# The softmax reciprocal is multiplied in on GpSimd instead of VectorE, in the attention of layer 0

## The reference

```python
s = where(valid, q @ k.T * dh ** -0.5 - slope * distance, NEG_INF)
p = exp(s - max(s));  den = sum(p);  o = (p @ v) / den     # per dilation group
out = sum over groups of softmax(m + log(den)) * o         # merged per head
```

## Time and profile before

| | |
|---|---|
| median of 3 runs | 1867.74 us |
| the profiled execution | 1868.67 us, span 1867.0 us |
| PE, PEld | 1716.0 us (92%), 1388.2 us (74%) |
| DVE, ACT, POOL | 1372.9 us (74%), 1087.9 us (58%), 51.4 us (3%) |
| mean granted TensorE clock | 0.973 |
| the units of the first half, of the second | from 173 to 215 us, from 325 to 370 us of the span |

### The profile page before, as it was taken

The page is one execution under the profiler, slowest core; times in us unless marked ns, Lnnn a source line. Parts: engine busy times, 40 slices in busy tenths (PEclk is TensorE's granted clock), DMA queues, the critical chain, the costliest instruction groups (busy, mean ns, idle before and its releaser), DMA issues. The chain is left out here.

```text
span 1867.0 us, 25871 instructions
## 1 busy us (share of the span) xinstructions
PE 1716.0 (92%) x9941; PEld 1388.2 (74%) x9941; DVE 1372.9 (74%) x1236; ACT 1087.9 (58%) x1074; POOL 51.4 (3%) x100
## 2 busy tenths in 40 slices
PE   0998998899999998989898999999999999999996
PEld 0997898679999875656676776767677766788784
DVE  4557556667776668559678887987988688898885
ACT  2344443553333345457766677777767678767773
POOL 2000000001111000000000000000000000000000
PEclk9998999899999999988899999999999999999998
DMA  9866177038887622249878998988999899999992
GB/s 298 300 236 227 58 259 261 11 123 284 311 293 260 226 83 88 84 156 360 314 288 312 336 357 296 394 317 319 364 342 365 293 351 359 385 346 340 364 346 90
DMA packets 244300, 503.84 MB, mean 270 GB/s; under 512 B 10296, under 2 KB 82144, under 8 KB 244192
## 3 DMA queue, kind: packets, MB, share of 16 engines
q1 hardware_dynamic: 228688, 451.44, 67.8%
q0 software_dynamic: 13824, 50.34, 7.3%
q10 hardware_dynamic: 1680, 0.60, 0.2%
HBM read 501.29 MB, written 1.05 MB: 269 GB/s over the span
## 5 line engine op out<-in xcount | busy, mean ns | idle before, releaser
L1404 DVE TENSOR_TENSOR wlo<-raw,whi 128x2048 fp32r<-128x2048 f32 x428 | 968.2, 2286 | 319.7 <-ACT whi L546 318.6
L546 ACT ACTIVATE whi<-raw 128x2048 fp32r<-128x2048 f32 x428 | 807.3, 1909 | 221.1 <-PE ps L863 85.5
L1225 PE MATMUL ps<-whi,ahi 128*128 128x512 f32 x896 | 300.5, 412 | 14.7 <-ACT whi L546 8.5
L1229 PE MATMUL ps<-wlo,ahi 128*64 128x512 f32 (+1 forms) x896 | 262.1, 400 | 16.6 <-DVE wlo L1404 16.5
L859 PE MATMUL ps<-ahi,whi 128*128 128x256 f32 x816 | 232.8, 285 | 2.0 <-DVE alo L1459 1.8
L863 PE MATMUL ps<-alo,whi 128*128 128x256 f32 x816 | 232.0, 284 | 0.0
L866 PE MATMUL ps<-ahi,wlo 128*128 128x256 f32 x816 | 231.8, 284 | 0.0
L1225 PEld LDWEIGHTS ps<-whi,ahi 128*128 128x128 f32 x896 | 167.9, 193 | 61.1 <-issue 24.5
L1229 PEld LDWEIGHTS ps<-wlo,ahi 128*64 128x64 f32 (+1 forms) x896 | 138.3, 157 | 91.2 <-DVE wlo L1404 28.3
L859 PEld LDWEIGHTS ps<-ahi,whi 128*128 128x128 f32 x816 | 157.5, 193 | 3.2 <-issue 3.0
L863 PEld LDWEIGHTS ps<-alo,whi 128*128 128x128 f32 x816 | 157.5, 193 | 0.3
(11 more groups left out here) (241 smaller groups left out, 2066.4 us busy)
## 6 DMA issues: line engine op xcount, KB each, us to landing
raw<-l_exp_w_gate SPq DMA_DIRECT2D x112, 1024.0 KB, 7.1
raw<-l_exp_w_up SPq DMA_DIRECT2D x112, 1024.0 KB, 7.9
raw<-l_exp_w_down SPq DMA_DIRECT2D x112, 1024.0 KB, 6.9
mraw<-mod_w POOLq DMA_DIRECT2D x96, 512.0 KB, 5.6
raw<-l_w_in SPq DMA_DIRECT2D x42, 1024.0 KB, 5.2
raw<-l_ffn_w_gate SPq DMA_DIRECT2D x14, 1024.0 KB, 5.5
raw<-l_ffn_w_up SPq DMA_DIRECT2D x14, 1024.0 KB, 6.9
raw<-l_ffn_w_down SPq DMA_DIRECT2D x14, 1024.0 KB, 6.4
```

The source lines that it names most:

```text
L546: act.activation(whi[s % SPL][:, :], raw[s % RAW][:, :], ACT.Copy).then_inc(hi_done, 1)
L1225: ins = pe.matmul(dst, stat, whi[s % SPL][:, a:a + BANK], start=start, stop=False, skip_group_check=True)
L1229: ins = pe.matmul(dst, stat, wlo[s % SPL][:, a:a + BANK], start=False, stop=stop, skip_group_check=True)
L1404: dve.tensor_tensor(wlo[s % SPL][:, :], raw[s % RAW][:, :], whi[s % SPL][:, :].bitcast(F32), ALU.subtract).then_inc(lo_done, 1)
```

## The change

The two products of step 4 go from VectorE to GpSimd; the reciprocal stays on VectorE. GpSimd waits for `rd_done` of the unit, multiplies in place, one instruction per head, and raises `pn_done`. So that the products find their place in GpSimd's program, its two loops over the vectors are written out, and the products of the first half stand between the fourth and the fifth DMA of vector 4, those of the second half ahead of the first DMA of vector 6. No other line is changed.

```diff
-            def fetch_vector(layer, v):
+            def fetch_vector(layer, v, tiles=range(KC)):
-                for kc in range(KC):
+                for kc in tiles:
                     waits(pool, mod_used, 48 * layer + 8 * v + kc - MRAW + 1)
                     src = dram["mod_w"][layer, kc * P:(kc + 1) * P, bass.ds(v * D, D)]
                     pool.dma_start(mraw[kc % MRAW][:, :], src).then_inc(mod_landed[kc % MRAW], 16)
-            fetch_vector(0, 0)
-            with pool.Fori(1, 6) as v:
-                fetch_vector(0, v)
-            with pool.Fori(0, 6) as v:
-                fetch_vector(1, v)
+            def divided(half, u):
+                pool.wait_ge(rd_done, 8 * half + u + 1)
+                for r in range(2):
+                    ins = pool.tensor_scalar(SB[u % 3][:, r, :], SB[u % 3][:, r, :], rden[:, 2 * u + r:2 * u + r + 1],
+                                             None, ALU.mult)
+                ins.then_inc(pn_done, 1)
+            for v in range(12):
+                if v == 6:
+                    for u in range(8):
+                        divided(1, u)
+                if v == 4:
+                    fetch_vector(0, v, range(MRAW))
+                    for u in range(8):
+                        divided(0, u)
+                    fetch_vector(0, v, range(MRAW, KC))
+                else:
+                    fetch_vector(v // 6, v % 6)
...
                         dve.reciprocal(rden[:, 2 * u:2 * u + 2], den[:, 2 * u:2 * u + 2]).then_inc(rd_done, 1)
-                        dve.wait_ge(rd_done, 8 * half + u + 1)
-                        for r in range(2):
-                            ins = dve.tensor_scalar(SB[u % 3][:, r, :], SB[u % 3][:, r, :],
-                                                    rden[:, 2 * u + r:2 * u + r + 1], None, ALU.mult)
-                        ins.then_inc(pn_done, 1)
```

## The result

| | before | after |
|---|---|---|
| median of six runs each | 1867.15 us (1863.61 to 1870.86) | 1875.37 us (1873.09 to 1876.86) |
| ratio, 95% interval | | 1.0045 (1.0033 to 1.0058) |
| the profiled execution | 1868.67 us, span 1867.0, clock 0.973 | 1876.86 us, span 1875.0, clock 0.971 |

The change costs 8.2 us. That is more than the 0.3% that I set as the bound of "same", so this is the case "slower", to which I had given 0.26. The time lies in the range (1865.3 to 1878) but not at the forecast (1869.7); it is where the rival *GpSimd's pair becomes the bound* stood with M = 3.0, at 1875.7 us. That the two agree so closely is in part luck, as the part on the prediction shows.

The account below looks back on a forecast made before the run. It took the attention units to be bound by a 7.33 us ring through ScalarE's PT copy, not VectorE. First units 0.8 + 0.9, turns 2 x 0.3, loops -0.3 gave +2.0: 1869.7 us, range 1865.3 to 1878.

Parts of the forecast that it names:

- the case "slower": Whole kernel: slower than before by over 0.3% (5.6 us); chance 0.26.
- GpSimd's pair becomes the bound: Rival in the attention units: GpSimd's two products outlast the room; 1875.7 us at M = 3.0, 1888 at 4.6; chance 0.22.
- M: Time of GpSimd's two products per attention unit: taken as 2.2 us, between 0.88 and 4.6.
- The ring and its room: Layer 0's attention: penalty, maximum, exponent, PT copy, transposes, scores take 7.33 us per two units; room for GpSimd's pair 2.1 us.
- The first unit: Start of each half's units: nothing hides GpSimd's pair; first transposes 1.65 us late, costing 0.9 and 0.8 us.
- Three turns a half: Transposes of units 2, 4 and 6 each pay the pair's excess over the room: 0.1 us each, 0.3 per half.
- The clock: TensorE's low clock behind gaps: shifted gaps may remove or add a slow stretch, 1.8 us either way.
- Contention: Rival: GpSimd's use of SB holds up VectorE's penalty and maximum; +14 us, 1882 us; chance 0.05.
- The written-out loops: GpSimd's vector fetches: each DMA may go 0.35 us sooner, counting only before the first projection; taken as -0.3 us.
- The DMAs and the last unit: mod_w tiles 48 to 51 go out near 357, some 60 us of cover, cost 0; last unit's product also covered.
- The products within the room: Rival: M at or under 2.1, the ring pays nothing; 1868.1 us at 1.5, 1867.1 at 0.88; chance 0.28.
- the forecast, up to M = 2.65: Main case: M from 2.1 to 2.65, +2.0 us, 1869.7 us; chance 0.41.

Follow-up runs that it names:

- e4: Kernel before, products still on VectorE, with ScalarE's PT copy moved ahead of its exponent: 1857.14 us beside 1866.02, ratio 0.9951.
- e2: Changed kernel with GpSimd's products over only 256 of a head's 512 columns, the rest undivided: 1862.81 us beside 1866.02 for the kernel before, ratio 0.9981.
- e8: Changed kernel with GpSimd's products over only 384 of a head's 512 columns, the rest undivided: 1868.54 us beside 1867.45 for the kernel before, ratio 1.0004.
- e11: Same kernel as e4 (kernel before, ScalarE's PT copy ahead of its exponent), run again: 1859.11 us beside 1867.16, ratio 0.9960.
- e7: Changed kernel with 12 idle TensorE products ahead of its wait for the even units' products: 1872.26 us beside 1867.45 for the kernel before, ratio 1.0025.
- e3: Changed kernel with one head's product on GpSimd and the other's back on VectorE: 1864.96 us beside 1866.02 for the kernel before, ratio 0.9994.
- e10: As e3, but GpSimd waits for VectorE's product instead of the reciprocal: 1866.22 us in one run, beside 1867.16 for the kernel before.
- e1: Kernel before with only GpSimd's two mod_w loops written out, products still on VectorE: 1867.06 us beside 1866.02, ratio 1.0000.

## Why the prediction was right or wrong

**The step that failed is the size of M.** The range held only since it reached up to M = 3.3, by a case to which I had given 0.22. I put M at 2.2 us "nearer to two" times VectorE's time for line 1534; it is 3.09, 1.56 an instruction, which is 2.4 times the 0.64 of line 1534 and 3.2 times the 0.49 of VectorE's own product. My argument by kinship was weak: the row nearest in kind was the product itself, and between 0.88 and 4.6 us for a pair I chose a value just at the edge where it would begin to matter. The Trainium skill's one-input figure (GPSIMD Engine Reference, Performance versus the Vector engine) is half of what the trace shows for the same 512 elements, 1.56 us against 769 ns; its two-input price scaled to 512 gave 1.12 us an instruction, too small as well. Here the measurement decides.

**With M right, the path is right, but the total agrees in part by luck.** By the steps of the prediction, M = 3.0 gave +8.3 - 0.3. Measured are 8.1 us of waits in the same links. But the first units cost 4.45 us (2.11 and 2.34) where the steps give 2.9, and the turns 3.7 (five of 0.71 to 0.75) where they give 5.4. And the units lost 11.65 us, of which 3.65 came back outside them; no term of the sum has either the 3.5 us of slow work or what came back.

- *The ring and its room.* Right. The ring was the copy's, the products a side branch (e4, e2). The room is 2.35 us by e8, where I had 2.1. The difference is the handoffs: VectorE to GpSimd takes 178.59 - 178.33 - 0.15 = 0.11 us, where I had taken 0.29 from a DMA, and GpSimd to TensorE 181.74 - 181.68 = 0.06 (0.07 in the second half), where I had 0.14. Without those 0.26 us the room would have been 2.1.
- *The first unit.* The transposes were 2.3 us later after their reciprocal (3.42 us instead of 1.13), which is the forecast 1.65 + 0.89 for M - 0.26 for the handoffs. What I let the clock give back in the second half did not come: I had the scores at the full clock since the mean of 334 to 337 was 0.83, but that rise came after TensorE had been at work from 331.31 on. After, TensorE stood idle for 4.97 us up to 338.25, the clock is 0.50 in the same stretch, and the scores at 340.14 took 2.08 us. I used the clock of a stretch as if it belonged to the time of day and not to the work. How long the low clock lasts there is not fixed by the kernel either: e4 and e11, which are the same, have 0.62 and 0.72 in 170 to 188. In the first half all 2.1 us reached unit 2 (191.47 against 189.37).
- *Three turns a half.* Right in the second half (0.75, 0.75, 0.71). In the first the low clock had covered one (5.86 us from penalty to transposes before, 5.87 after) and two paid.
- *The clock.* I had priced it at 1.8 us either way. In the units it cost 3.5, and outside there was less of it, worth 2 to 3 us. Net it is of the size that I wrote, but by two movements of which I foresaw neither. e7 shows the first by taking it away; the second is seen in one pair of stretches and otherwise only added up, and that the change caused it is not shown.
- *Contention.* The rival that VectorE's penalty and maximum would grow is wrong: the median of a penalty instruction is 680 ns in both kernels, beside a busy POOL. Between two products it exists (e3, e10), 0.3 us for the one that starts later.
- *The written-out loops.* The handoff shrank as said: in straight code 24.41 + 1.28 = 25.69 to 25.99 is 0.30 us, in the loop it was 0.64. It was worth nothing: the first reciprocal stands at 178.33 against 178.35, and e1 is 1.0000. The -0.3 of the sum was 0.
- *The DMAs and the last unit.* Right in cost. The four tiles went out at 368.22, 11 us later than I had written, and VectorE used the first at 434.20. The last unit's transposes (214.55) wait for nothing.

What was badly placed were the chances. The products within the room and the forecast, up to M = 2.65, had 0.69 together; everything I knew of M lay between 0.88 and 4.6, and with the time flat below 2.1 and rising by 6 us and more for each us above, the upper half of that interval decides, and I gave it 0.22.

## What to carry to other kernels

Work that moves to a slower engine is free only within the slack that its branch has in the ring; read that slack from the orders of time (here 2.35 us per unit), and if the price of the new engine isn't in the trace, treat the break-even price as the thing to be bet on. A nearly full engine in a stretch where TensorE waits isn't the bound if the wait ends elsewhere: taking 0.9 of 3.7 us off VectorE gave nothing, while exchanging two blocks on ScalarE, with no work removed, gave 8 us. And a longer gap of TensorE can cost twice, once as a wait and once as slow work behind it, but only where TensorE's work is what the others wait for.

## What the runs showed of the hardware

- GpSimd's `tensor_scalar` in fp32 with a per-partition scalar takes 0.92, 1.24 and 1.56 us for 256, 384 and 512 columns on 128 partitions; VectorE's takes 0.49 for 512. I had not expected a factor of 3.2.
- Semaphore handoffs to and from GpSimd's arithmetic are short, 0.11 and 0.06 us; to a DMA that GpSimd issues it is 0.30 us in straight code and 0.64 in a loop over a register.
- Two `tensor_scalar` in SBUF on VectorE and GpSimd at once: the one that starts later grows, GpSimd's by 0.3 us (e3, overlap 0.43), VectorE's by 0.25 (e10, overlap 0.46). A penalty with its second operand in PSUM, and a reduction, leave GpSimd's 1.56 us as they are.
- The same gap of TensorE can be followed by a fall of the clock or not. The gap of 0.25 us was in e4 and not in e11, which is the same kernel. In e3 TensorE waits 2.12 us ahead of the transposes of unit 6 in both halves; the values behind them took 1.98 us in the first half and 1.09 in the second. So a low stretch that is there in one execution and not in another isn't yet an effect of the change.
